# Feed-forwards in three parts, 30 more shared units, and two of four weight sums by an adding DMA

## What is computed

```python
def swiglu(x, w_gate, w_up, w_down):
    return (jax.nn.silu(x @ w_gate) * (x @ w_up)) @ w_down      # 2048 -> 5632 -> 2048
h = h + 0.5 * swiglu(rms_norm(h, ffn1_norm), ffn1_w_gate, ffn1_w_up, ffn1_w_down)
...
h = h + 0.5 * swiglu(rms_norm(h, ffn2_norm), ffn2_w_gate, ffn2_w_up, ffn2_w_down)
```

## Time and profile before

| | us |
|---|---|
| median of 3 runs | 2217.98 |
| profiled execution | 2217.39 |
| its span | 2215.3 |
| PE busy | 2202.3 (99%), 9899 matmuls |
| DVE busy | 1409.5 (64%) |
| ACT busy | 1073.8 (48%) |
| POOL busy | 39.4 (2%) |
| moved by DMA | 425.68 MB, 192 GB/s on the mean |

### The profile page before, as it was taken

The page is one execution under the profiler, slowest core; times in us unless marked ns, Lnnn a source line. Parts: engine busy times, 40 slices in busy tenths (PEclk is TensorE's granted clock), DMA queues, the critical chain, the costliest instruction groups (busy, mean ns, idle before and its releaser), DMA issues.

```text
span 2215.3 us, 24399 instructions
## 1 busy us (share of the span) xinstructions
PE 2202.3 (99%) x9899; PEld 1817.2 (82%) x9899; DVE 1409.5 (64%) x1432; ACT 1073.8 (48%) x1183; POOL 39.4 (2%) x71
## 2 busy tenths in 40 slices
PE   9999999999999999999999999999999999999998
PEld 7888888888888888877777888888888888888886
DVE  5988645688755544445655665788864568875555
ACT  6545443454544444454444545464543346444454
POOL 0000000000010000010010000000000000000000
PEclk9999999999999999999999999999999999999999
DMA  8655555654555666655555665655546665556664
GB/s 288 239 176 193 179 190 186 233 214 173 190 179 187 200 193 195 180 174 169 175 170 161 186 186 180 232 205 180 201 171 190 190 237 200 186 182 198 190 190 143
DMA packets 165705, 425.68 MB, mean 192 GB/s; under 512 B 11592, under 2 KB 11600, under 8 KB 150368
## 3 DMA queue, kind: packets, MB, share of 16 engines
q1 hardware_dynamic: 163840, 419.21, 58.1%
q0 software_dynamic: 1472, 4.70, 0.8%
q10 hardware_dynamic: 288, 0.30, 0.0%
HBM read 422.06 MB, written 2.11 MB: 191 GB/s over the span
## 4 chain that ended last, share of the span: by engine, by line
PE 98%; DMA 1%; issue 0%; DVE 0%; ACT 0%; ACTq 0%; POOLq 0%; POOL 0%
PE acc L1493 18%; PE acc L1495 18%; PE acc L1494 18%; PE acc L1536 6%; PE acc L1538 6%; PE acc L1537 6%; PE turn L1538 4%; PE turn L1536 4%; PE turn L1537 4%; PE fox L1538 4%; PE fox L1537 4%; PE fox L1536 4%; PE turn L1513 1%; DMA raw<-in_ffn_up 0%; PE acc L1530 0%; PE turn L1787 0%
## 5 line engine op out<-in xcount | busy, mean ns | idle before, releaser
L1025 DVE TENSOR_TENSOR w_lo<-raw,w_hi 128x1024 fp32r<-128x1024 f32 x451 | 558.0, 1240 | 585.1 <-ACT w_hi L594 584.6
L594 ACT ACTIVATE w_hi<-raw 128x1024 fp32r<-128x1024 f32 x451 | 477.1, 1060 | 682.9 <-PE acc L1495 643.0
L1493 PE MATMUL acc<-w_hi,x_both 128*128 128x512 f32 x940 | 371.0, 395 | 0.8 <-DVE x_both L1188 0.8
L1495 PE MATMUL acc<-w_hi,x_both 128*128 128x512 f32 x940 | 366.6, 390 | 0.0
L1494 PE MATMUL acc<-w_lo,x_both 128*128 128x512 f32 x940 | 366.3, 390 | 0.0
L1493 PE MATMUL acc<-w_hi,slab_r 128*128 128x512 f32 x832 | 325.5, 391 | 0.0
L1495 PE MATMUL acc<-w_hi,slab_r 128*128 128x512 f32 x832 | 324.2, 390 | 0.0
L1494 PE MATMUL acc<-w_lo,slab_r 128*128 128x512 f32 x832 | 324.0, 389 | 0.0
L1493 PEld LDWEIGHTS acc<-w_hi,x_both 128*128 128x128 f32 x940 | 176.6, 188 | 42.5 <-issue 5.7
L1495 PEld LDWEIGHTS acc<-w_hi,x_both 128*128 128x128 f32 x940 | 176.5, 188 | 37.4
L1494 PEld LDWEIGHTS acc<-w_lo,x_both 128*128 128x128 f32 x940 | 176.7, 188 | 35.2
(11 more groups left out here) (432 smaller groups left out, 3513.6 us busy)
## 6 DMA issues: line engine op xcount, KB each, us to landing
raw<-in_ffn_w_down SPq DMA_DIRECT2D x176, 512.0 KB
raw<-in_ffn_up SPq DMA_DIRECT2D x50, 1024.0 KB, 4.9
raw<-in_w_in SPq DMA_DIRECT2D x96, 512.0 KB
lo_raw<-in_ffn_up SPq DMA_DIRECT2D x42, 1024.0 KB, 4.9
raw<-in_w_merge_gate SPq DMA_DIRECT2D x64, 512.0 KB
more<-in_ffn_up SPq DMA_DIRECT2D x25, 1024.0 KB, 4.9
raw<-in_ffn_up SPq DMA_DIRECT2D x33, 512.0 KB, 3.9
raw<-in_w_out SPq DMA_DIRECT2D x32, 512.0 KB
```

What stands on the lines that cost most here:

```text
L594: nc.scalar.activation(w_hi[:, slot, :, :], raw[:, slot, :, :], ACT.Copy).then_inc(hi_split, 1)
L1025: nc.vector.tensor_tensor(w_lo[:, slot, :, :], raw[:, slot, :, :], w_hi[:, slot, :, :].bitcast(F32), ALU.subtract).then_inc(lo_split, 1)
L1493: nc.tensor.matmul(to, hi(kt)[:, tok], w_hi[:, slot, k, :], start=kt == 0, stop=False)
L1495: last = nc.tensor.matmul(to, lo(kt)[:, tok], w_hi[:, slot, k, :], start=False, stop=kt == BK * nb - 1)
```

## The change

1. A feed-forward is now one list of 17 pairs (ffn_pairs): parts of 4, 4 and 3 up pairs, each followed by two down pairs of 1024 columns. The down projections are made of the same items as the up pairs, and two of their units (HS) can be shared. Every pair but the first made in this way is shared.
2. In a stage the B items alternate with plain ones: B S B S B S S A A A S for up, B S B S S S S A A (A) S for down.
3. ring_order skips a slot of a ring at fixed item numbers, so that the rings end where the next phase begins.
4. Of the four weight sums of a shared unit, ACT negates the two tiles they start from (negate, three items ahead of the A), POOL adds the other columns' tiles from HBM onto them with an accumulating DMA, and DVE makes the remaining two.
5. The sums for shared units of a down pair are made from the hidden rows (hid_full, hid_hi, hid_lo in free slabs).
6. The last two units of a feed-forward are multiplied column half by column half, and the rows of the next norm are turned earlier. The last norm's tiles are kept in y_r, and the embedding and gains in the room of x_both; the rounding of the thin weights is moved from the start of the projection to behind its seventh group; p and the final gain are loaded at two moments.

```diff
-HALF_KT = (24, 20)
+PARTS = (4, 4, 3)
...
+def ffn_pairs():
+    pairs, j = [], 0
+    for part, ups in enumerate(PARTS):
+        kt0 = 4 * sum(PARTS[:part])
+        pairs += [Pair("up", part, j + n, UNITS, 4 * n) for n in range(ups)]
+        pairs += [Pair("down", part, n, 2 * ups, kt0) for n in range(2)]
+        j += ups
+    return pairs
+PAIR = ffn_pairs()
+PAIRS = len(PAIR)
+LAST_UP = [i for i in range(PAIRS - 1) if PAIR[i].kind == "up" and PAIR[i + 1].kind == "down"]
+def shared_units(ffn, i):
+    if i <= FIRST[ffn] or i >= PAIRS:
+        return 0
+    return US if PAIR[i].kind == "up" else HS
...
+def stage_of(ffn, i):
+    b, a = shared_units(ffn, i), shared_units(ffn, i + 1)
+    plain = [("S", i, u) for u in range(b, PAIR[i].units)]
+    own = []
+    for u in range(b):
+        own.append(("B", i, u))
+        if len(plain) > 2:
+            own.append(plain.pop(0))
+    own += plain
+    if a:
+        own = [*own[:-1], *[("A", i + 1, u) for u in range(a)], own[-1]]
     return own
...
+def sum_made_at(i):
+    return 4 if PAIR[i].part == len(PARTS) - 1 else 2
+def turned_at(stage):
+    return 4 if len(stage) >= 10 else 3
...
+def ring_order(count, size, first):
+    skips = (size - 1 - first - (count - 1)) % size
+    order, at = [], first
+    for n in range(count):
+        if n in (30, 60, 90, 120)[:skips]:
+            at += 1
+        order.append(at % size)
+        at += 1
+    return order
...
+        quads = ring_order(len(kinds), QUADS, 2 if name == "ffn1" else 0)
+        slots = ring_order(sum(kind != "B" for kind in kinds), TALL, 4 if name == "ffn1" else 0)
...
+            def add_second_columns(name, w_up, w_down):
+                for it in shared_items(name):
+                    pool.wait_ge(negated, it.step)
+                    pool.dma_start(tall(name, it.raw, 0)[:, 1:3, :], second_columns(it, w_up, w_down), accum_op=ALU.add)\
+                        .then_inc(added[it.raw], 16)
...
+            def negate(name, it):
+                act.wait_ge(tall_full[it.raw], 16 * it.raw_count)
+                q = tall(name, it.raw, 0)
+                nc.scalar.activation(q[:, 1, :], q[:, 0, :], ACT.Copy, scale=-1.0)
+                nc.scalar.activation(q[:, 2, :], q[:, 2, :], ACT.Copy, scale=-1.0).then_inc(negated, 1)
...
+            def turn_hidden(name, pair):
+                for ct in range(2):
+                    t = UP_TURN[name] + 2 * PAIR[pair].n + ct
+                    act.wait_ge(turned, t + 1 - TURNS["x"])
+                    kt, bank = PAIR[pair].kt0 + 2 * ct, banks_of(name, pair)[2 * ct][:, :].rearrange("p (k c) -> p k c", k=2)
+                    if kt < BK * HS:
+                        nc.scalar.activation(hid_full[:, kt // BK, :, :], bank, ACT.Copy)
+                    nc.scalar.activation(slab_r[:, kt:kt + 2, :], bank, ACT.Copy).then_inc(turned_hi, 1)
+            def feed_forward(name, normed, hi, gain, rows=None, p_turn=False):
                 for n, stage in enumerate(STAGES[name]):
+                    i = FIRST[name] + n
                     for k, it in enumerate(stage):
                         split_item(name, it)
+                        if k + 3 < len(stage) and stage[k + 3].kind == "A":
+                            negate(name, stage[k + 3])
+                        if k == 0 and shared_units(name, i):
+                            copy_parts(name, i)
+                        if k == 1 and i > 0 and PAIR[i - 1].kind == "up":
+                            if i == 1:
+                                act.wait_ge(rstd_done, normed)
+                            silu(stage[0].at, name, i - 1)
                         if k == 1 and n == 0 and rows:
                             rows()
+                        if n == 0 and 3 <= k <= 5:
+                            split_sums(name, i + 1, k - 3)
+                        if k == turned_at(stage) and i > 0 and PAIR[i - 1].kind == "up":
+                            turn_hidden(name, i - 1)
+                        if i + 1 in LAST_UP and k == sum_made_at(i) + 1:
+                            split_sums(name, i + 2, 0)
+                        if i in LAST_UP and k == 3:
+                            split_sums(name, i + 1, 1)
+                        if i == PAIRS - 1 and k == 3:
+                            if p_turn:
+                                turn_plain(TURN["p"], TURN["p"] % 2, p_hi)
+                            turn_rows("down" + name[-1], 0, hi, gain)
+                        if i == PAIRS - 1 and k == 5:
+                            turn_rows("down" + name[-1], 1, hi, gain)
...
+                dve.wait_ge(trio_full[it.trio], 16 * it.trio_count)
+                q, later = tall(name, it.raw, 0), later_tiles(name, it.trio, 0)
                 w21, w22 = later[0][:, 0, :], later[0][:, 1, :]
                 t4 = later[0][:, 2, :] if len(later) == 1 else later[1][:, 0, :]
-                after_own(nc.vector.tensor_tensor(q[:, 1, :], q[:, 2, :], q[:, 0, :], ALU.subtract))
-                nc.vector.tensor_tensor(q[:, 2, :], w22, q[:, 2, :], ALU.subtract)
+                dve.wait_ge(added[it.raw], 16 * ADDED_COUNT[it.step])
                 after_own(nc.vector.tensor_tensor(q[:, 3, :], w22, q[:, 1, :], ALU.subtract))
                 nc.vector.tensor_tensor(t4, w21, q[:, 3, :], ALU.subtract).then_inc(steps_made, 1)
...
+            def feed_forward(name, hi, lo, next_hi, next_lo, gain, first_rows=None, later_rows=None, p_turn=False):
                 for n, stage in enumerate(STAGES[name]):
+                    i = FIRST[name] + n
                     for k, it in enumerate(stage):
                         if k + 1 < len(stage) and stage[k + 1].kind == "A":
                             make_steps(name, stage[k + 1])
                         split_item(name, it)
                         if k == 0 and n == 0 and first_rows:
                             first_rows()
+                        if k == 0 and shared_units(name, i):
+                            combine(name, i)
+                        if k == 1 and i > 0 and PAIR[i - 1].kind == "up":
+                            hidden_out(name, i - 1)
+                        if k == 1 and i > 0 and PAIR[i - 1].kind == "down":
+                            dve.wait_ge(multiplied, stage[0].at)
+                            for ct in range(2):
+                                add_rows(2 * PAIR[i - 1].n + ct, banks_of(name, i - 1)[2 * ct:2 * ct + 2], 0.5)
                         if k == 1 and n == 0 and later_rows:
                             later_rows()
+                        if n == 0 and 3 <= k <= 5:
+                            split_sums(name, i + 1, k - 3)
+                        if n == 0 and 2 <= k <= 4:
+                            make_sums(name, i + 1, k - 2, hi, lo)
+                        if k == turned_at(stage) and i > 0 and PAIR[i - 1].kind == "up":
+                            turn_hidden(name, i - 1)
+                        if i + 1 in LAST_UP and k == sum_made_at(i):
+                            make_sums(name, i + 2, 0)
+                        if i + 1 in LAST_UP and k == sum_made_at(i) + 1:
+                            split_sums(name, i + 2, 0)
+                        if i in LAST_UP and k == 2:
+                            make_sums(name, i + 1, 1)
+                        if i in LAST_UP and k == 3:
+                            split_sums(name, i + 1, 1)
+                        if i == PAIRS - 1 and k == 3:
+                            if p_turn:
+                                turn_plain(TURN["p"], TURN["p"] % 2, p_hi, p_lo)
+                            turn_rows("down" + name[-1], 0, next_hi, next_lo, gain)
+                        if i == PAIRS - 1 and k == 5:
+                            turn_rows("down" + name[-1], 1, next_hi, next_lo, gain)
+                dve.wait_ge(half_done, 1 if name == "ffn1" else 2)
+                add_rows(2, banks_of(name, PAIRS - 1)[0:2], 0.5)
...
+            def feed_forward(name, x_pair, first_rows=None, p_turn=False):
+                down_turn = "down" + name[-1]
                 for n, stage in enumerate(STAGES[name]):
+                    i = FIRST[name] + n
+                    primed = shared_units(name, i) > 0
+                    hidden_turned = UP_TURN[name] + 2 * PAIR[i - 1].n + 2 if i > 0 and PAIR[i - 1].kind == "up" else None
+                    if primed:
+                        pe.wait_ge(combined, ADDED[name, i])
                     for k, it in enumerate(stage):
+                        operand = x_pair if PAIR[it.pair].kind == "up" else hidden_of
+                        pe.wait_ge(lo_split, it.at + 1)
+                        if it.kind == "A":
+                            if it.unit == 0 and i > 0:
+                                pe.wait_ge(read_out, GROUP[name] + 2 * i)
+                                if hidden_turned:
+                                    pe.wait_ge(turned_lo, hidden_turned)
```

(81 more changed lines are left out.)

505 lines of the change are left out of this document (223 added, 282 removed).

## The result

The changed kernel takes 2326.1 us (median of 4 runs, 2318.7 to 2335.6) against 2218.0 us of the kernel before (4 runs as well, not 3 as in its table): a ratio of 1.049 (95% interval 1.044 to 1.053), slower by 108 us. My forecast was 2216.5 and my range ended at 2243.

The account below looks back on a forecast made before the run. PE was taken as the bound, matmul count setting the time: 2217.4 less 20.4 for 90 matmuls plus 19.2 of stalls gave 2216.2, rounded to 2216.5 us; eight-in-ten range 2205 to 2243.

Parts of the forecast that it names:

- the new chain: Shared unit's weight sums: load, ACT negation, POOL's adding DMA, DVE's sums and split; 9.1 us plus the add's time.
- L: Time from the negated tile to the added one, by POOL's 512 KB adding DMA: taken as 6.2 us.
- the load: SP's load of a shared unit's weight tile, at the head of its sums: landing taken as 4.0 us.
- my stalls: PE's waits for late weight tiles in the feed-forwards: 10.2 in six stages plus 9.0 behind ring skips, 19.2 us.
- 90 matmuls at 0.2266 us: Shared units in the feed-forwards: 30 more, each saving 3 matmuls, take 20.4 us off PE.
- No engine becomes a bound, combining costs nothing: DVE about 1495 us, ACT about 1230; combining after 31 stages hides under the last plain unit, with 1.4 us of cover.
- Stalls behind the ring's skips: ACT's queue where ring_order skips a slot: negation waiting for a late load delays splits, 9.0 us together.
- the fast end: POOL's adding DMA landing in 5.3 us or less, say 5.0: 12 us of stalls, 2209 us; chance 0.31.
- slow adds: Rival: adding DMA reads both operands and shares engines with SP's loads; at 7.5 us, 41 us of stalls, 2238; chance 0.25.
- thirteen up-to-up stages: Stages from up pair to up pair: 15.6 us of room for the weight sums, so no stall forecast.
- the three with two A: Stages with two shared first halves: at least 16.3 us of room for the weight sums, no stall forecast.
- the six tight ones: First stage of each feed-forward and four from down to up: 13.6 us of room, 1.7 us stall each, 10.2 together.

Follow-up runs that it names:

- e1: Changed kernel without negation and adding DMA, DVE making all four weight sums: 2202.3 us, ratio 0.993 to the kernel before; 2201.5 us when repeated in more runs.
- e2: Changed kernel with the negation kept and the adding DMA left out, so sums lack the other columns' tiles: 2209.0 us, ratio 0.9962 to the kernel before.
- e7: Changed kernel with one of the two sums by the adding DMA (256 KB) and the other by DVE: 2236.1 us, ratio 1.008 to the kernel before.
- e3: Changed kernel with POOL's DMA of the same 512 KB as a plain overwriting copy instead of an addition: 2237.3 us, ratio 1.0099 to the kernel before.
- e5: Changed kernel with all sums by DVE, the last sum of a pair's third shared unit repeated 12 times more: 2370.6 us, ratio 1.0693.
- e9: Changed kernel with all sums by DVE, the last sum of a pair's third shared unit repeated 5 times more: 2242.3 us, ratio 1.0113.

## Why the prediction was wrong, step by step

Three steps failed, all in the price of the new chain: L was taken too short, the load was taken as it is without adds beside it, and a stall was priced at its own length alone. L at 8.2 in place of 6.2 raises my stalls from 19.2 to 56 us (+37), with the rest of the waits they are 86.8 (+30), and PE's slower work behind them comes on top (+45). Together that is 112 of the 114 us between my 2216.2 and the 2330.7 of the profiled execution.

- **90 matmuls at 0.2266 us: right.** e1 is busy for 19.7 us less than the kernel before, with 20.4 forecast.
- **No engine becomes a bound, combining costs nothing: right.** No wait of PE in either kernel is for `combined`, and without the adding DMA DVE even hides two more sums a unit (e1).
- **Stalls behind the ring's skips, 9.0: right.** One of about 5 us was forecast near 200 us; it is 4.74 long at 227.6, in e2 4.7. All of e2's three are 7.2.
- **L, the term that was mis-sized: 6.2 taken, 8.2 measured** in the median, 6.7 to 10.5 by tile and weight. I put the line for 512 KB between two plain transfers, and let the second operand count as a reason against the fast end only. The 1024 KB row that I kept as the upper end was the nearest one, as e7 shows from the other side: an add of 256 KB lands as a plain 512 KB. My "slow adds" rival had this part of the mechanism, but with L = 8.2 it gives 56 us of stalls and 2253, still 73 us short.
- **The load at 4.0: too small where it counts.** Over all 81 first halves it is still 4.0 in the median (3.8 in e1). But where a pair has three A, the first of them loads in 3.8 and A2, the one that the stall hangs on, in 5.9, with the adds of the units in front in flight; in the stage shown it is 6.4. I had said that an SP load falls on top of the add, but not that adds fall on top of SP's loads. With each stage's own load and add for A2 in place of my 4.0 and 6.2, my sum can be held against the rows. In the thirteen up-to-up stages, which I had put at nothing, it gives 44.1 us, and PE waited 45.0 between A2's load and A1, no stage off by more than 0.6; in the three with two A, 4.4 against 4.5; in the six tight ones 33.3 against 28.9, where 2.1 of the difference lie in the very first. So the counting of the ring was sound, and two numbers put into it were not.
- **The clock: a term that wasn't there.** I costed a stall at its own length. 39 stalls cost 86.8 us as waits and, beside e1, another 44 us of PE's busy time, most of it matmuls at the lower clock. The clock stood at half for 76.8 us in all, part of it while PE still waited (6.0 before). The Trainium skill ("TensorE: Matmul & The Clock Gate", Part 1) gives N/1.2 GHz from start to start for a cold array, 427 ns for 512 columns; the trace agrees, with 0.43 us. I had the column of the clock before me at 1.00 in every stretch but the last and read it as a constant. The last row was the hint: 0.69 in the 11 us in which PE is busy for 0.93. Even with the right stalls I would have written 2217.4 - 20.4 + 87 = 2284.

The fit that I weighed beside the rows was too low as well: the Trainium skill's line ("DMA: Bandwidth & Descriptors", Anatomy of one DMA) gives an estimate of 3.2 us for 512 KB issued by GpSimd, and even plain transfers take 4.7 here in the median (e3), 4.0 at the least.

**What stays open.** An add has twice the engine time of a plain transfer (3.2 against 1.57 us), which alone would make 4.7 into some 6.3, by my estimate; 8.2 were measured. That the rest is the shared engines, whose share is 0.93 to 1.01 in such a stretch, is argued and not isolated: an adding DMA in a quiet stretch, or onto tiles that nobody waits for, wasn't tried. Nor is it settled how the 28 us of e3 divide between longer loads and the wait for the plain transfer itself.

## What to carry to other kernels

Work that leaves a hidden engine for a DMA isn't free when the DMA stands in a chain with a deadline: count from the moment the buffer comes free, with landing times as they are under load, and an adding DMA as one of twice its bytes. Here DVE had the room (72% with all sums) and the ring had not. Where the slack is 2 us, as it was here, a new step of 8 us can't be hidden. And once PE waits for several us at a time, the matmuls behind the wait run slower as well: price such a stall at its length and 1 to 2 us more (44 us for 39 waits in the changed kernel, 43.5 for 21 longer ones in e5).

## What the runs showed of the hardware

- An accumulating DMA of 512 KB from HBM onto SBUF costs 3.2 us of all 16 engines and 272 packets; the plain one 1.57 us and 144. It lands 8.2 us after issue in the median, the plain one 4.7, one of 256 KB 4.8.
- It also slows its neighbours: where three shared units follow one another, the last one's load of 512 KB takes 5.9 us in the median in the changed kernel and 3.8 in e1. The first one's, ahead of the adds, takes 3.8 in both.
- POOL needs 1.09 us (up) or 1.20 us (down) in the median to issue the add of 512 KB, 0.86 for 256 KB, and 0.72 for the plain 512 KB.
- PE's matmuls started 0.43 us apart (1.2 GHz) behind the waits of 2.46 us (at 1444.69 in e9) and 4.24 us (at 383.62 in the changed kernel), and the second cost up to 2.4 us beyond its length; behind one of 1.03 us it stayed at 0.23 (2.4 GHz). Of three waits of 2.95 us in e9 one was followed by slow matmuls and two were not. In PE's busy time above e1, 21 waits cost 43.5 us (e5), 39 cost 44.3 (changed), 14 cost 13.5 (e9).
